# Top-k pick in sparse attention: the last places taken by match-and-replace instead of a compare chain for ties

## What is computed

```python
def dsa_block(q, qi, wi, limit, k, v, ki, top_k):
    s = jnp.einsum('bthd,bsd->bths', qi.astype(jnp.float32), ki.astype(jnp.float32))
    score = jnp.einsum('bth,bths->bts', wi.astype(jnp.float32), jax.nn.relu(s))
    visible = jnp.arange(L)[None, :] < limit[:, None]
    score = jnp.where(visible[None], score, -jnp.inf)
    top_val, top_idx = lax.top_k(score, top_k)
    ...
```

## Time and profile before

| | us |
|---|---|
| median of 3 runs | 3,713.04 |
| lowest and highest run | 3,710.76 and 3,717.03 |
| span of the profiled execution (first to last instruction; its own time is given as this span) | 3,702.1 |
| PE busy | 3,263.2 |
| DVE busy | 2,260.1 |
| ACT busy | 1,078.5 |
| POOL busy | 785.9 |

### The profile page before, as it was taken

The page is one execution under the profiler, slowest core; times in us unless marked ns, Lnnn a source line. Parts: engine busy times, 40 slices in busy tenths (PEclk is TensorE's granted clock), DMA queues, the critical chain, the costliest instruction groups (busy, mean ns, idle before and its releaser), DMA issues. The chain is left out here.

```text
span 3702.1 us, 51508 instructions
## 1 busy us (share of the span) xinstructions
PE 3263.2 (88%) x19482; PEld 2934.2 (79%) x19482; DVE 2260.1 (61%) x4788; ACT 1078.5 (29%) x1854; POOL 785.9 (21%) x404
## 2 busy tenths in 40 slices
PE   3999985787888887888789999999979899999997
PEld 2777764566666665667689999999969899999997
DVE  5667672777777766684226656656531666666654
ACT  2222222455455544444212221221221211211221
POOL 0000002111000000000245433433214434434420
PEclk7999996999999998999889999999989899999999
DMA  4122225221111010000321111111132211111101
GB/s 138 63 93 84 76 86 151 55 55 33 49 28 28 28 28 25 14 15 13 114 86 35 57 45 34 57 45 34 33 113 75 69 35 45 57 34 45 57 11 48
DMA packets 164909, 202.67 MB, mean 55 GB/s; under 512 B 27775, under 2 KB 138660, under 8 KB 162596
## 3 DMA queue, kind: packets, MB, share of 16 engines
q1 hardware_dynamic: 164772, 200.90, 17.2%
HBM read 155.61 MB, written 45.25 MB: 54 GB/s over the span
## 5 line engine op out<-in xcount | busy, mean ns | idle before, releaser
L1642 DVE SCALAR_TENSOR_TENSOR ffn_gv<-ffn_up,ffn_taps,ffn_gv 128x1056 f32<-128x1056 f32 (+2 forms) x264 | 418.5, 1599 | 157.0 <-ACT ffn_gv L1595 150.6
L1663 DVE TENSOR_TENSOR feed_hT<-feed_hT,ffn_ps_d 128x352 f32<-128x352 f32 x528 | 275.3, 522 | 329.1 <-PE ffn_ps_d L1548 329.1
L1535 PE MATMUL ffn_ps_u<-feed_nhi,feed_up_hi 128*128 128x352 f32 x2112 | 459.7, 326 | 15.8 <-DVE feed_nlo L1673 11.0
L1535 PE MATMUL ffn_ps_u<-feed_nhi,feed_up_lo 128*128 128x352 f32 x2112 | 456.6, 324 | 0.0
L1535 PE MATMUL ffn_ps_u<-feed_nlo,feed_up_hi 128*128 128x352 f32 x2112 | 456.2, 324 | 0.0
L1535 PEld LDWEIGHTS ffn_ps_u<-feed_nhi,feed_up_hi 128*128 128x128 f32 x2112 | 360.9, 190 | 19.3 <-DVE feed_nlo L1673 12.4
L1548 PE MATMUL ffn_ps_d<-ffn_a_hi,ffn_down_hi 128*128 128x352 f32 x1056 | 343.9, 326 | 29.3 <-DVE ffn_a_lo L1654 24.0
L1535 PEld LDWEIGHTS ffn_ps_u<-feed_nhi,feed_up_lo 128*128 128x128 f32 x2112 | 363.8, 188 | 0.0
L1535 PEld LDWEIGHTS ffn_ps_u<-feed_nlo,feed_up_hi 128*128 128x128 f32 x2112 | 360.2, 188 | 0.0
L862 POOL TENSOR_SCALAR att_diag<-ident,keep_w 128x128 f32<-128x128 f32 (+1 forms) x136 | 79.6, 606 | 1310.7 <-PE att_ps_s L892 800.6
L1548 PE MATMUL ffn_ps_d<-ffn_a_lo,ffn_down_hi 128*128 128x352 f32 x1056 | 343.0, 325 | 0.0
(11 more groups left out here) (258 smaller groups left out, 5964.5 us busy)
## 6 DMA issues: line engine op xcount, KB each, us to landing
feed_raw_up<-in_w_up SPq DMA_DIRECT2D x44, 1024.0 KB, 4.9
scratch_sT<-proj_sT SPq DMA_DIRECT2D x16, 1472.0 KB, 5.2
ffn_raw_down<-in_w_down SPq DMA_DIRECT2D x22, 1024.0 KB, 4.9
feed_nlo<-scratch_mixT SPq DMA_DIRECT2D x16, 528.0 KB, 7.7
proj_x<-in_x_prompt SPq DMA_DIRECT2D x16, 512.0 KB, 4.7
att_qi<-scratch_sT SPq DMA_DIRECT2D x16, 512.0 KB, 3.6
att_qa<-scratch_sT SPq DMA_DIRECT2D x16, 512.0 KB, 5.2
att_qb<-scratch_sT SPq DMA_DIRECT2D x32, 256.0 KB, 5.8
```

Of the source, the lines that this page charges most:

```text
L1535: ins = pe.matmul(ps_u[:, half, s, 0:SUB], a[:, q, k, :], b[:, k, SUB * s:SUB * s + SUB], start=(k == 0 and n == 0), stop=(k == KC - 1 and ...
L1642: ins = dve.scalar_tensor_tensor(gv[:, half, lo:hi], up[:, lo + shift + j - 2:hi + shift + j - 2], taps[:, 2 * j + half, e:e + 1], gv[:, h ...
L1663: dve.tensor_tensor(at, at, ps_d[:, j % 2, 0:SUB], ALU.add).then_inc(partial_read[j % 2], 1)
```

## The change

The last places are no longer found by value and tie, but by overwriting. `place` + 1 of the eight largest scores left are wanted. `take_next` makes eight values out of the eight largest: a wanted one stays, from another 1e38 is taken away, so that it matches nothing. One match-and-replace writes -1e30 over the first position of each wanted value in `work`. After that every score taken holds about -1e30, and one compare (`leave_out_rest`) makes the mask: -1e30 where `work` is above -0.5e30. The hidden columns of the first 64 rows hold -2e38, are not above that limit and get their mask by a memset. A row has failed if `place` is above 7 (`failed`, L1091); then `more_places` takes eight more, and a row with `place` above 15 goes to `take_largest` as before. The table `falling` and its load are gone.

```diff
-        KEY_LOADS, TABLE_LOADS, Q_LOADS = 6, 3, 6
+        KEY_LOADS, TABLE_LOADS, Q_LOADS = 6, 2, 6
...
-            sp.dma_start(falling[:, :], t["falling"].broadcast_to([P, SEQ])).then_inc(tables_loaded, 16)
...
                     st.step(dve.tensor_tensor(low_work, low_work, row, ALU.add))
-                    st.step(dve.max(top[0:T, :], low_work))
                     st.step(dve.tensor_scalar(col(place), col(above), -1.0, b.keep - 1.0, ALU.mult, ALU.add))
-                    st.step(dve.tensor_scalar(col(missing), col(place), 7.0, None, ALU.min))
-                    st.step(dve.scalar_tensor_tensor(chosen[0:T, 0:8], places[0:T, 0:8], col(missing), top[0:T, :], ALU.is_equal, ALU.mult))
-                    st.step(dve.tensor_reduce(col(kth), chosen[0:T, 0:8], AX.X, ALU.add))
+                    take_next(b, st, 0)
                 elif part == HALVINGS + 3:
-
-                    st.step(dve.tensor_scalar(chosen[0:T, 0:8], top[0:T, :], col(kth), None, ALU.is_gt))
-                    st.step(dve.tensor_reduce(col(reached), chosen[0:T, 0:8], AX.X, ALU.add))
-                    st.step(dve.tensor_tensor(col(missing), col(place), col(reached), ALU.subtract))
-
-                    st.step(dve.scalar_tensor_tensor(low_work, row, col(kth), falling[0:T, 0:S], ALU.is_equal, ALU.mult))
-                    st.step(dve.max(lowest[0:T, 0:8], low_work))
+                    leave_out_rest(b, st)
+                    st.step(dve.tensor_scalar(col(failed), col(place), 7.5, None, ALU.is_gt))
                 else:
-                    keep_to_tie(b, st, 8)
                     with dve.If(failed_rows(st) > 0):
-                        more_ties(b)
+                        more_places(b)
...
+            def take_next(b, own, start):
+
+                T, left = b.T, work[0:b.T, 0:b.S]
+                own.step(dve.max(top[0:T, :], left))
+                own.step(dve.tensor_scalar(wanted[0:T, :], places[0:T, start:start + 8], place[0:T, 0:1], NEVER, ALU.is_gt, ALU.mult))
+                own.step(dve.tensor_tensor(wanted[0:T, :], top[0:T, :], wanted[0:T, :], ALU.subtract))
+                own.step(dve.match_replace(left, wanted[0:T, :], left, -FAR))
+
+            def leave_out_rest(b, own):
 
                 T, S = b.T, b.S
...
+                own.step(dve.tensor_scalar(mask[0:T, b.n % 2, 0:S], work[0:T, 0:S], -0.5 * FAR, MASKED, ALU.is_gt, ALU.mult))
+                if not b.sample:
+                    own.step(dve.memset(mask[0:CHUNK, b.n % 2, S - CHUNK:S], MASKED))
...
-            def more_ties(b):
-
-                T, S = b.T, b.S
-                at, order = mask[0:T, b.n % 2, 0:S], work[0:T, 0:S]
+            def more_places(b):
+
                 own = Steps(dve, tie_steps)
-                own.step(dve.match_replace(at, lowest[0:T, 0:8], order, 0.0))
-                own.step(dve.max(lowest[0:T, 8:16], at))
-                keep_to_tie(b, own, 16)
+                take_next(b, own, 8)
+                leave_out_rest(b, own)
+                own.step(dve.tensor_scalar(failed[0:b.T, 0:1], place[0:b.T, 0:1], 15.5, None, ALU.is_gt))
                 total = failed_rows(own)
```

More of the change, by code:

```diff
@@ L50 @@
 FAR = 1.0e30
+NEVER = 1.0e38
 UNSEEN, TAKEN, TAKEN_BELOW = -2.0e38, -3.0e38, -2.5e38
@@ L710, in phase_attend @@
         halves, places = m.sb("halves", [P, HALVINGS]), m.sb("places", [P, 16])
-        falling, lowest, chosen = m.sb("falling", [P, SEQ]), m.sb("lowest", [P, 16]), m.sb("chosen", [P, 16])
-        missing, last_tie = m.sb("missing", [P, 1]), m.sb("last_tie", [P, 1])
+        wanted = m.sb("wanted", [P, 8])
         far, low, spread, back = m.sb("far", [P, HALVINGS + 1]), m.sb("low", [P, 1]), m.sb("spread", [P, 1]), m.sb("back", [P, 1])
-        bound, above, place, kth = m.sb("bound", [P, 1]), m.sb("above", [P, 1]), m.sb("place", [P, 1]), m.sb("kth", [P, 1])
-        reached = m.sb("reached", [P, 1])
+        bound, above, place = m.sb("bound", [P, 1]), m.sb("above", [P, 1]), m.sb("place", [P, 1])
         failed, failedT, failures = m.sb("failed", [P, 32]), m.sb("failedT", [P, 32]), m.sb("failures", [P, 1], I32)
@@ L1102, in pick @@
+                    st.step(dve.tensor_scalar(col(failed), col(place), 7.5, None, ALU.is_gt))
                 else:
-                    keep_to_tie(b, st, 8)
                     with dve.If(failed_rows(st) > 0):
-                        more_ties(b)
+                        more_places(b)
                     dve.memset(idle[:, :], 0.0).then_inc(scores_taken, 1)
                     dve.wait_ge(scores_taken, b.n + 1)
-            def keep_to_tie(b, own, found):
-                T, S = b.T, b.S
[L1113 to L1118, removed]
+            def take_next(b, own, start):
[4 more added lines that the diff above has]
+                own.step(dve.match_replace(left, wanted[0:T, :], left, -FAR))
@@ L1818, in constants @@
     places = np.broadcast_to(np.arange(16, dtype=f), (P, 16))
-    return {"halves": halves.astype(f), "places": places.astype(f), "falling": np.arange(SEQ, 0, -1, dtype=f)[None], "rope_table": np.concatenate(table, 1).astype(f), "band": np.array(band, f), "band_first": np.array(first, f),
+    return {"halves": halves.astype(f), "places": places.astype(f), "rope_table": np.concatenate(table, 1).astype(f), "band": np.array(band, f), "band_first": np.array(first, f),
             "band_old": np.array(old, f)}
```

## The result

| us | before | after |
|---|---|---|
| median of 4 runs each | 3,711.90 | 3,792.33 |
| lowest and highest | 3,707.54, 3,717.03 | 3,791.49, 3,801.36 |
| span of the profiled execution | 3,702.1 | 3,799.6 |

The changed kernel takes 1.0219 times the time of before (95% interval 1.0204 to 1.0234), some 80 us more. The forecast was 3,804, its range 3,783 to 3,833.

The account below looks back on a forecast made before the run. PE waits for DVE's end of each pick at block turns. Savings of 59 us against 150 added by `take_largest` gave net +91 on a span of 3,702.1, 3,793, plus 11 around it: 3,804 us, range 3,783 to 3,833.

Parts of the forecast that it names:

- The first rival: Block 13: the row has 15 places or fewer on the chip, `take_largest` never runs, 3,654 us; chance 0.07.
- Both signs: 31 rounds on 1792 columns between 1,400 and 1,600 us; PE waiting some 160 us before one L920.
- Points 1 and 2: End of each pick: some 60 us of DVE saved over 15 blocks, of which PE sees 32 us at turns.
- Point 3: Match-and-replace ahead of L1164 delays memory head's exponentials; blocks 2 to 6 still give 5.9 us, large blocks hide it.
- the sign that I had named against it: Blocks 8 to 15: if PE's wait for ACT's exponentials grows there, point 3 is wrong.
- The second rival: Forward step exposed in large blocks too, no clock back: savings shrink from 59 to 37 us, time 3,826; chance 0.10.
- Point 4: Block 7, second case before and after: second pass saves 1.2 us, common part 3.7, together 4.9 us.
- Point 5: Block 13: 7.3 us saved, `take_largest` adds 150 us (137 to 157), 31 rounds of 4.65 us.
- The third rival: Each turn of the `take_largest` loop fetches code, 0.34 us a round, 11 us more, 3,815; chance 0.05.
- Point 6: Start of attention, table `falling` no longer loaded: 4.0 us saved, between 1.8 and 4.2.
- Its sign: Start of attention: DVE's first memset at about 599.5 us.
- Point 7: Granted clock behind removed PE waits: up to 1.3 us a turn, 0 to 9 over seven turns, 5 taken.

Follow-up runs that it names:

- the first experiment: Changed kernel plus a third set of eight for rows with 16 to 23 places to go, ahead of `take_largest`: 3,658.22 us, 0.9847 of before.
- the second experiment: Kernel before, with one compare changed so that block 13 runs `take_largest` under the old pick too: 3,859.39 us, 1.0389 of before.
- the fourth experiment: The first experiment with the match-and-replace of the first eight moved behind the memory slot's maxima: 3,648.60 us, 0.9817 of before.
- the third experiment: The first experiment with the unused `falling` table and its load put back: 3,661.00 us, 0.985 of before.
- the fifth experiment: The fourth experiment with the failure flags summed on DVE, so one count is fetched instead of four: 3,642.67 us, 0.9808 of before.
- the sixth: The fifth experiment with all of part 13 behind the memory slot's maxima in the picks of blocks 2 to 6: 3,631.23 us, 0.9778 of before.

## Why the prediction came out as it did

**The sign and its reason were right.** `take_largest` ran once, in block 13, 31 rounds on 1792 columns, and every other large block got faster. This came from evaluating the scores, not from the profile; the profile of before only let the count of second cases be compared. The first rival (no fallback, 3,654) is what the first experiment built with a detour: 3,658. Both signs named for it came: 31 rounds in that block, and a wait of PE of 154.6 us where some 160 were named.

**Points 1 and 2** had the mechanism right. From the max to the wait's end the pick of block 10 took DVE 15.5 us and takes 10.6; 0.3 of the 4.9 is a shorter wait, so 4.6 against 4.5 forecast. (The terms of point 1 add up to two L1100's and 0.9, not 1.1; it changes little.) At the turns into blocks 8 to 12 and 14 no wait of PE for DVE of 0.8 us or more is left, at 15 it is 1.70.

**Point 3 failed.** "Of the second wait, 2.08 us there, 1.5 stay won", and 5.9 us over blocks 2 to 6: the five turns came out 2.5 us longer in the changed kernel and 2.6 in the first experiment. Against the second experiment's 245.8 us for the old code they are 0.7 shorter; a gain of 5.9 is in neither comparison. The waits of PE from 600 to 970 us show why, before and then after:

```profile
PE att_ps_o L965 <- DVE att_rows L1191: 25.0, 8, 12.3
PE att_ps_l L920 <- ACT att_probs L1024: 17.2, 7, 3.5
PE att_ps_o L965 <- ACT att_pT L799: 11.2, 16, 1.2
```

```profile
PE att_ps_l L918 <- ACT att_probs L1022: 21.4, 7, 4.3
PE att_ps_o L963 <- ACT att_pT L798: 16.8, 21, 1.2
PE att_ps_o L963 <- DVE att_rows L1182: 9.6, 4, 6.7
```

Block 7's own wait (12.3, now 6.7) taken off, the wait for DVE's rows fell from 12.7 to 2.9, by 9.8 us. The wait for the exponentials rose by 4.2, about the 4 us that the prediction's sum had set against the gain. What it left out stands in the next two sums. The wait for ACT's copies of transposed probabilities rose by 5.6, 4.4 of it inside the five stretches: in the second slot the copies were late next, behind the rows, and at block 2 they left 1.18 of the 2.08 us. They are not the forward step's doing: with the step undone in the fourth experiment this wait was no shorter (15.7 us, 14.6 in the first experiment). And PE's busy time over the five stretches rose by 4.1 us, from the 200.72 shown here to 204.82, at a granted clock of 0.94 and not 0.96:

```profile
659.29:901.87 242.58, 200.72 (x1150) 154.32 (x1149) 192.53 (x644) 124.21 (x296) 23.38 (x40) 0.96 0.20 52
```

4.4 and 4.1 make up the 8.4 us between the forecast of -5.9 and the measured +2.5, as far as single traces carry it. In the large blocks the delay was hidden, as point 3 has it: the sign that I had named against it, a longer wait for exponentials in blocks 8 to 15, did not come (of 4.9 us more from 600 to 1900 us, 4.2 lie before 970). The second rival, which had it exposed there as well, falls. Its 37 us of savings should have read 39 (59 - 15 - 5), thus 3,824.

**Point 4**, block 7: 4.9 us predicted, 4.8 measured.

**Point 5**, block 13: the fallback at 150 us measured 146, the stretch as a whole +137.9 where +142.7 was forecast. The round was 4.54 and not 4.65 us; at its turn DVE stood idle 0.38 us, not 0.45. The third rival (a fetch in each round, 0.34 us more, thus 4.99) falls, since the rounds are shorter than 4.65 and not longer. Between the match-and-replace of one round and the max of the next stand two register operations beside the branch; what each has of the 0.38 us isn't shown. The Trainium skill (Advanced Engine Details and Errata, Control Flow Timing) gives 0.11 us for the compare-and-branch. A forecast by that figure alone would have been 30 x 0.27 = 8 us short, an estimate from that page and this row.

**Point 6**: 4.0 us forecast, 3.0 in the change and 3.1 in the third experiment. Its sign, DVE's first memset at about 599.5 us, did not come (606.09), since all of the attention starts later; against PE's first logits it is 1.9 us sooner, where 1.8 was forecast.

**Point 7**, the clock, was mis-sized: 5 us, between 0 and 9. Seven turns gained 42.7 us where 29.3 of waits were to go, so 13 us came with them. The windows of the stretches into blocks 8 to 12 show where they come from (columns as in the earlier trace rows), before and in the first experiment:

```profile
1049.57:1130.77 81.20, 71.89 (x396) 54.15 (x396) 58.12 (x152) 40.71 (x79) 4.68 (x8) 0.96 0.12 32
...
1216.60:1309.70 93.10, 82.39 (x470) 63.84 (x469) 65.29 (x151) 47.30 (x88) 4.68 (x8) 0.96 0.10 28
...
sum 437.85, PE 384.88 PEld 295.41 DVE 309.39 ACT 220.98 POOL 23.39; mean PE 76.98 PEld 59.08 DVE 61.88 ACT 44.20 POOL 4.68
```

```profile
1046.23:1121.73 75.50, 68.75 (x396) 51.88 (x395) 54.16 (x145) 40.53 (x80) 4.66 (x8) 1.00 0.13 34
...
1203.23:1289.01 85.78, 79.53 (x468) 61.87 (x467) 60.82 (x146) 47.20 (x89) 4.66 (x8) 1.00 0.11 30
...
sum 408.18, PE 374.51 PEld 289.09 DVE 288.35 ACT 221.21 POOL 23.29; mean PE 74.90 PEld 57.82 DVE 57.67 ACT 44.24 POOL 4.66
```

The same matmuls took 384.9 us of PE and take 374.5, at a granted clock of 0.96 to 0.98 before and 1.00 now. That is 10.4 us over five turns, two a turn; I had read at most 1.3 a turn from a window of 4 us behind one wait, which ended before the clock was back. The other 3 us lie in blocks 14 and 15, where PE's busy time fell by 3.6. At the last turn, into the sample block, PE's wait of 3.28 us is 0.92: 2.4 us of the 2.7 that were to go.

**The sum.** By the traces: -43 for seven turns, +2.5, -4.8, +138, -5.8 at the start and -2.4 at the last turn make +85 us, against +91 forecast: 8 us claimed in the small blocks and not gained cancelled 8 us too few in the large ones, which was luck; of the 6 us left, 5 are block 13's. The -5.8 at the start are 3.0 of point 6 and some 3 that the first experiment's trace, with the same code, does not have. The runs say 80, their interval 76 to 87, which holds the traces' sum; what is left between 80 and 85 is no more than the spread of the runs. The 11 us that I took "for what lies around the span" was misnamed: that is 1.8 us, and the rest is that the profiled execution of before ended sooner than the runs shown. The sum was added to the median, so this did no harm. The difference of the two spans, 97.5, is no measure of the change either: 6.7 us of it lie ahead of the attention, and from the turn into the sample block to the last mark the changed kernel's profile has 49.7 us where before has 44.7, 4.9 us more where 2.4 less were due.

## What to carry to other kernels

When a fast path takes over a condition from the code it replaces, count on the real data how often it fails: a fallback that never ran before cost 146 us in one of fifteen blocks, more than the shorter path gave in all of them. One more step of the fast path in front of it kept the gain. A wait that is taken away pays only up to the next one in the same slot, so ask what is late next behind it in the same slot, and what the moved step delays; in a chain of in-order engines, put whatever nobody waits for behind what the busiest engine waits for. And where short idle spells of PE go, look at its busy time under the lower granted clock as well: here some 13 us came beside 29 of waits in the large blocks, and in the small ones the clock took 4 back.

## What the runs showed that I had not expected

In the profiled execution of the changed kernel the granted clock fell to half in the middle of the sample block, with PE busy over 18 of 20 us. The windows, after and before:

```profile
1840.00:1860.00 20.00, 18.06 (x78) 12.75 (x78) 5.03 (x26) 4.99 (x16) 0.00 (x0) 0.50 0.00 1
```

```profile
1746.00:1766.00 20.00, 16.63 (x108) 11.94 (x108) 7.29 (x38) 7.25 (x23) 0.00 (x0) 0.86 0.00 1
```

0.50 is 1.2 GHz, and 78 matmuls kept PE busy for longer than 108 had before. The stretch that begins with the turn into the sample block lasted 49.7 us where the first experiment needed 41.4; the fifth experiment's profile shows 49.6 there and the sixth 41.0, with the same work. Over that stretch the granted clock was 0.66 in the changed kernel and the fifth experiment, 0.88 in the first and the sixth, and 0.96 in the fourth, which took 39.2 us. Each kernel has one trace, so whether this goes with the kernel or with the execution isn't shown, and the cause stays open. The profiled run, 3,801.36 us, lies above the other three by about these 8 us, which speaks for the execution. But the fifth experiment's profiled run has the same 8 us in it and is the fastest of its four.

Fetching a count from memory into DVE's sequencer is dearer than it looks: four fetches with their sum kept DVE waiting 3.4 to 3.9 us at the turns. One fetch leaves 1.24 us at the turn into block 10, which is still more than the whole new compare (0.89 us on 1408 columns).
